# Second block's neighbourhood attention: TensorE's work on two tiles put together, VectorE's and GpSimd's finishing steps moved later

## The chip, the core and the metric

The kernel runs on one core of a Trainium2 chip. The core has five engines that run their own instruction streams in order and meet at semaphores: TensorE (PE, matrix products; PEld in the profile is its weight load), VectorE (DVE), ScalarE (ACT), GpSimd (POOL) and SyncE (SP, which only starts transfers here). The metric is the device time of one execution in microseconds (us), less is better.

## The reference, cut to what matters

Two blocks follow each other over 512 tokens of width 1024. The first (sparse attention beside a state-space mixer) isn't touched. The second has two layers; in each, 1024 columns of output are made by two attentions, a differential one (`out_b`) and a neighbourhood one (`out_a`), gated, and multiplied by `w_out`:

```python
def neighborhood_attention(q, k, v, rpb):   # 8 heads of 64, grid of 8 rows x 64 columns
    ...
        logits = jnp.einsum('bhcd,bhicjd->bhcij', qr, kr).astype(jnp.float32) * scale + bias[None]
        p = jax.nn.softmax(logits.reshape(b, h, GRID_W, wr * NA_WIN_C), axis=-1)
        ...
        return jnp.einsum('bhcij,bhicjd->bhcd', p, vr)
...
    y = jnp.concatenate([out_a * jax.nn.silu(g_a), out_b * jax.nn.silu(g_b)], axis=-1)
    x = x + y @ w_out[l]
```

Each query sees a window of 8 x 16 neighbours. The change concerns how `out_a` is worked through, and what stands around the start of `y @ w_out[l]`.

## The kernel before

**Tiles.** The neighbourhood attention of a layer is cut into 16 tiles (`PAIRS_NA`, `N_NA`): tile m is a block of 128 queries (i = m % 4) of a pair of heads (p = m // 4), each head with a window of 256 keys. One tile passes through six steps on four engines:

- scores (`na_score`, TensorE): per head three products, since q and k are kept as a high and a low part (`q_hi`, `q_lo`, `k_hi`, `k_lo`). The two heads lie on rows 0 to 63 and 64 to 127 of the array (64*128 in the trace). They go to two of four banks (`S_BANKS`), so that scores m wait until tile m-2 has been taken.
- take (`na_take`, VectorE): adds the bias and finds the maximum, into `prob2` (called `ring` in the trace). It waits for the bias of its pair of heads, which GpSimd's queue loads (`load_bias`).
- exponentials (`na_exp`, ScalarE), two per tile, then the reciprocal of the sums (`na_inverse`, VectorE) and the scaling (`na_scale`, GpSimd).
- turn (`na_turn`, TensorE, L1542 in the trace, 128*128): four transposes into bank 0 or 1; the move (`na_move`, ScalarE) takes them to `probT2` (`soft` in the trace).
- values (`na_weigh`, TensorE, 128*64): the products with v. The trace records eight for a tile, and names v `xn_t` or `v` according to the block. Two tiles, a *group* g, share a bank.
- products and low part: `na_out` (VectorE) multiplies a group by its gate twice, once rounded into `hT_hi` and once in full; `na_lo` (GpSimd) makes the rest, `hT_lo`. TensorE's products with `w_out` read both.

**Order.** Every engine's order is written out by hand. Tiles 0 to 2 (`N_EARLY`) are scored and taken while the last projections still run. From tile 3 on, TensorE does in step j: scores j, turn j-3 (`NA_LAG`), values j-4. VectorE does take j, reciprocal j-1, on odd j from 7 the products of group (j-7)//2, and on j = 6, 8, 10, 12 the low part of a quarter of the other attention's result (`mixT_lo`, L2161). ScalarE does move j-3, exponentials j, and on j = 4, 6, 8, 10 the high part of that quarter (`mixT_hi`). GpSimd scales tile m, and on even m from 6 makes the low part of group m//2 - 3; the last three low parts follow the last scale.

**End of the stage.** After step 16 TensorE does the first half of output tile 0 (`out_rows(0, 6, ...)`: twelve products that need the other attention only and the bank of tile 14's scores), then turn 14, values 13, turn 15, values 14 and 15, and the first half of output tile 1. Then it waits for `na_lo` of all groups (L1642) and does the second halves.

## Time and profile before

| | us |
|---|---|
| three runs | 935.77, 937.44, 937.67 |
| median | 937.44 |
| profiled execution | 937.15 |
| its span, first to last instruction | 935.3 |
| mean granted TensorE clock | 0.997 |

Busy in that span: PE 899.6 us (96%), PEld 707.5, DVE 578.1, ACT 449.5, POOL 116.9. The stage that the change touches runs twice, about 562 to 596 us and about 857 to 890 us into the span. How to read the rows: a time is the start, the number after it the duration in us; "x4" is the number of instructions merged in the row; a bracket at the end gives the idle time of the engine before the row and what ended it. A matmul's duration is longer than its pitch, since the engine overlaps them; the distance from one start to the next is what a step costs.

### The profile page before, as it was taken

To read this page: it belongs to the slowest core of one execution; us is meant where nothing else is said; L and a number is where in the kernel's file an instruction comes from. 1 tells how busy PE (TensorE), PEld (TensorE's weight loads), DVE (VectorE), ACT (ScalarE), POOL (GpSimd) and SP (SyncE) were. 2 spreads that over 40 slices of the span, in tenths; PEclk is the share of its full clock that TensorE was granted. 3 is DMA by queue.
4 is the path that set the end of the run, shared out by engine and by line. 5 is a ranking of instruction groups with operands and counts; after the bars stand their busy time and mean duration, and the time that the engine had idled before them with its cause. 6 is when DMAs were issued, how large, how long until landed. Compare 5 with 4: busy or idle time off the path is not lost.

```text
span 935.3 us, 14659 instructions
## 1 busy us (share of the span) xinstructions
PE 899.6 (96%) x5733; PEld 707.5 (76%) x5733; DVE 578.1 (62%) x1168; ACT 449.5 (48%) x962; POOL 116.9 (12%) x137
## 2 busy tenths in 40 slices
PE   3999999999999999999999999999999999999996
PEld 1679888774667788887788886788887778887785
DVE  5899798988886472438953447245255975335633
ACT  4634324566785243426925349234333863535731
POOL 1001120005300010000010017200000010002702
PEclk9999999999999999999999999999999999999998
DMA  9735636266000332322204334123242222323103
GB/s 381 314 99 131 187 137 181 102 187 242 22 2 1 113 128 92 113 90 88 90 22 138 105 94 133 43 90 91 90 138 95 78 91 90 90 90 120 62 23 90
DMA packets 34646, 104.69 MB, mean 112 GB/s; under 512 B 14929, under 2 KB 14929, under 8 KB 32146
## 3 DMA queue, kind: packets, MB, share of 16 engines
q1 hardware_dynamic: 28098, 85.77, 27.9%
q0 software_dynamic: 3824, 15.73, 5.3%
q10 hardware_dynamic: 2656, 2.26, 0.9%
q8 instruction: 46, 0.75, 0.3%
q14 instruction: 22, 0.18, 0.1%
HBM read 98.37 MB, written 4.19 MB: 110 GB/s over the span
## 4 chain that ended last, share of the span: by engine, by line
PE 88%; DVE 4%; ACT 3%; DMA 2%; issue 2%; POOL 0%; SPq 0%; POOLq 0%; DVEq 0%; ACTq 0%
PE bank L1043 81%; PE bank L1383 2%; PE bank L1403 2%; PE bank L1542 1%; DMA ring<-in_w_ada 1%; DMA bias_ring<-in_na_bias 1%; PE bank L1459 1%; DVE arena L1670 0%; PE bank L1449 0%; ACT ring L855 0%; ACT w_hi L903 0%; ACT arena L736 0%; DVE soft L2133 0%; DVE soft L2111 0%; DVE xn_t L2176 0%
## 5 line engine op out<-in xcount | busy, mean ns | idle before, releaser
L2156 DVE TENSOR_TENSOR w_lo<-ring,w_hi 128x1024 fp32r<-128x1024 f32 x80 | 97.8, 1225 | 114.6 <-ACT w_hi L903 111.6
L1043 PE MATMUL bank<-w_hi,hT_hi 128*128 128x512 f32 x320 | 125.6, 392 | 1.3 <-issue 1.0
L1043 PE MATMUL bank<-hT_hi,w_hi 128*128 128x512 f32 x320 | 126.2, 395 | 0.0
L1043 PE MATMUL bank<-w_lo,hT_hi 128*128 128x512 f32 x320 | 124.7, 390 | 0.0
L1043 PE MATMUL bank<-hT_hi,w_lo 128*128 128x512 f32 x320 | 124.6, 389 | 0.0
L1043 PE MATMUL bank<-hT_lo,w_hi 128*128 128x512 f32 x320 | 124.6, 389 | 0.0
L1043 PE MATMUL bank<-w_hi,hT_lo 128*128 128x512 f32 x320 | 124.5, 389 | 0.0
L903 ACT ACTIVATE w_hi<-ring 128x1024 fp32r<-128x1024 f32 x80 | 84.4, 1058 | 11.6 <-PE bank L1043 11.4
L1043 PEld LDWEIGHTS bank<-w_hi,hT_hi 128*128 128x128 f32 x320 | 60.1, 188 | 15.1 <-issue 2.9
L1043 PEld LDWEIGHTS bank<-hT_hi,w_hi 128*128 128x128 f32 x320 | 60.1, 188 | 14.0 <-issue 0.7
L1043 PEld LDWEIGHTS bank<-hT_lo,w_hi 128*128 128x128 f32 x320 | 60.1, 188 | 12.7
L1043 PEld LDWEIGHTS bank<-w_lo,hT_hi 128*128 128x128 f32 x320 | 60.1, 188 | 12.7
L1043 PEld LDWEIGHTS bank<-w_hi,hT_lo 128*128 128x128 f32 x320 | 60.1, 188 | 12.1
L1043 PEld LDWEIGHTS bank<-hT_hi,w_lo 128*128 128x128 f32 x320 | 60.1, 188 | 12.0
L908 ACT ACTIVATE bank<-x_t 128x512 f32<-128x512 f32 x24 | 14.5, 602 | 95.7 <-DVE x_t L2361 62.2
L566 POOL TENSOR_TENSOR ring<-ring,small 128x512 f32<-128x512 f32 x32 | 35.5, 1115 | 165.3 <-DVE small L2257 164.9
L855 ACT ACTIVATE ring<-ring,small 128x512 f32<-128x512 f32 x64 | 45.6, 714 | 13.9 <-DVE small L2101 11.4
L1043 PE MATMUL bank<-arena 128*64 128x64 f32 (+5 forms) x608 | 51.0, 293 | 0.3 <-PE bank L1043 0.2
L2101 DVE CUSTOM_DVE_ANT_0 ring<-bank,bias_ring 128x512 f32<-128x512 f32 x64 | 41.2, 685 | 0.0
L1043 PEld LDWEIGHTS bank<-arena 128*64 128x64 f32 (+1 forms) x608 | 31.3, 147 | 11.4 <-issue 10.2
L974 ACT ACTIVATE q_hi<-bank 128x512 fp32r<-128x512 f32 x16 | 9.6, 598 | 60.2 <-PE bank L1043 60.2
L2312 DVE SCALAR_TENSOR_TENSOR q_lo<-bank,q_hi 128x512 fp32r<-128x512 f32 x16 | 11.1, 692 | 43.2 <-ACT q_hi L974 43.2
(321 smaller groups left out, 1804.1 us busy)
## 6 DMA issues: line engine op xcount, KB each, us to landing
ring<-in_w_units SPq DMA_DIRECT2D x80, 512.0 KB, 3.7
ring<-in_w_ada SPq DMA_DIRECT2D x4, 2048.0 KB, 10.5
bias_ring<-in_na_bias POOLq DMA_DIRECT2D x8, 1024.0 KB, 5.4
ring<-in_w_out SPq DMA_DIRECT2D x2, 2048.0 KB, 8.6
bias_ring<-in_t_bias POOLq DMA_DIRECT2D x8, 448.0 KB, 3.7
x_t<-in_x SPq DMA_DIRECT2D x4, 512.0 KB, 5.7
arena<-in_w_ada SPq DMA_DIRECT2D x1, 2048.0 KB, 19.9
arena<-in_w_ada SPq DMA_DIRECT2D x2, 1024.0 KB, 22.8
```

The costliest lines, as they stand in the source:

```text
L566: pool.tensor_tensor(p, p, r, MUL).then_inc(S["na_scaled"], 1)
L855: act.activation(p, p, ACT.Exp, scale=-1.0, bias=negm[:, k % 8:k % 8 + 1], accum_out=ssum[:, k % 8:k % 8 + 1])\
L903: act.activation(w_hi[:, u % 4], raw_w[:, u % 4], ACT.Copy).then_inc(S["w_hi_ready"], 1)
L908: settle(act.activation(place[:, 0:n], x[:, i, c0:c0 + n], ACT.Square, scale=scale, accum_out=ssq[:, part * NT + i:part * NT + i + 1]))
L974: act.activation(q_hi[:, t, :], src[:, :], ACT.Copy, scale=SCALE).then_inc(S["qk_hi"], 1)
L1043: return pe.matmul(out, lhsT, rhs, start=first, stop=last)
L1383: ins = pe.transpose(bank[u % 2][:, b * P:(b + 1) * P], src[:, b * P:(b + 1) * P], ident)
L1403: ins = pe.transpose(bank[k % 2][:, b * P:(b + 1) * P], prob1_of(k)[:, b * P:(b + 1) * P], ident)
L1459: ins = pe.transpose(bank[ROW_BANKS[i][b]][:, k * P:(k + 1) * P], xn[:, i % 2, (4 * b + k) * P:(4 * b + k + 1) * P], ident)
L2101: dve.tensor_tensor_reduce(prob_of(k)[:, 0:width], bank[S_BANKS[k % 4]][:, 0:width], bias, -scale, 3.0e38, ADD, MIN, negm[:, k % 8:k % 8 + ...
L2156: dve.tensor_tensor(w_lo[:, u % 4], raw_w[:, u % 4], w_hi[:, u % 4].bitcast(fp32), SUB).then_inc(S["w_split"], 1)
L2312: dve.scalar_tensor_tensor(lo_[:, t, :], bank[(pt2(l, g) + t) % 4][:, :], SCALE if isq else 1.0, hi_[:, t, :].bitcast(fp32), MUL, SUB).the ...
```

## The change

Nothing is computed otherwise; four orders are altered, in both layers.

```diff
@@ GpSimd
                     na_scale(l, m)
-                    if m >= 6 and m % 2 == 0:
-                        na_lo(l, m // 2 - 3)
-                for g in range(N_NA // 2 - 3, N_NA // 2):
+                    if m >= 10 and m % 2 == 0:
+                        na_lo(l, m // 2 - 5)
+                for g in range(N_NA // 2 - 5, N_NA // 2):
                     na_lo(l, g)
@@ TensorE
-                        for j in range(N_EARLY, N_NA + NA_LAG + 1):
-                            if j < N_NA:
-                                na_score(l, j)
-                            if j <= N_EARLY + 1:
-                                pe.wait_ge(S["proj_evac"], pt2(l, 8) - 1 + j - N_EARLY)
-                            if j < N_NA + NA_LAG:
-                                na_turn(l, j - NA_LAG)
-                            if j > N_EARLY:
-                                na_weigh(l, j - NA_LAG - 1)
-                            if j == N_NA:
-                                out_rows(0, 6, range(0, 4))
+                        na_score(l, N_EARLY)
+                        pe.wait_ge(S["proj_evac"], pt2(l, 8) - 1)
+                        na_turn(l, 0)
+                        pe.wait_ge(S["proj_evac"], pt2(l, 8))
+                        for j in range(N_EARLY + 1, N_NA, 2):
+                            na_score(l, j)
+                            na_score(l, j + 1)
+                            for m in (j - NA_LAG, j + 1 - NA_LAG):
+                                na_turn(l, m)
+                            for m in (j - NA_LAG - 2, j - NA_LAG - 1):
+                                if m >= 0:
+                                    na_weigh(l, m)
+                        na_turn(l, N_NA - 3)
+                        na_turn(l, N_NA - 2)
+                        na_weigh(l, N_NA - 5)
+                        na_weigh(l, N_NA - 4)
+                        out_rows(0, 6, range(0, 4))
+                        na_turn(l, N_NA - 1)
+                        for m in (N_NA - 3, N_NA - 2, N_NA - 1):
+                            na_weigh(l, m)
                         out_rows(1, 7, range(0, 4))
@@ VectorE
-                            if j >= 7 and j % 2:
-                                na_out(l, (j - 7) // 2)
+                            if j >= 8 and j % 2 == 0:
+                                na_out(l, (j - 8) // 2)
                             ...
                         na_inverse(l, N_NA - 1)
-                        for g in range(N_NA // 2 - 3, N_NA // 2):
+                        for g in range(N_NA // 2 - 4, N_NA // 2):
                             na_out(l, g)
```

TensorE in the middle of the stage: before, one tile's scores, one turn, one tile's values, and the next scores.

```order
L1043 MATMUL bank<-k_hi,q_hi 128x256 x2
L1043 MATMUL bank<-k_hi,q_lo 128x256 x2
L1043 MATMUL bank<-k_lo,q_hi 128x256 x2
L1542 MATMUL bank<-cons,ring 128x128 x4
L1043 MATMUL bank<-soft,xn_t 64x128 x4
L1043 MATMUL bank<-k_hi,q_hi 128x256 x2
```

After, scores of two tiles, two turns, values of two tiles:

```order
L1043 MATMUL bank<-k_hi,q_hi 128x256 x2
L1043 MATMUL bank<-k_hi,q_lo 128x256 x2
L1043 MATMUL bank<-k_lo,q_hi 128x256 x2
L1043 MATMUL bank<-k_hi,q_hi 128x256 x2
L1043 MATMUL bank<-k_hi,q_lo 128x256 x2
L1043 MATMUL bank<-k_lo,q_hi 128x256 x2
L1542 MATMUL bank<-cons,ring 128x128 x8
L1043 MATMUL bank<-soft,v 64x128 x8
L1043 MATMUL bank<-k_hi,q_hi 128x256 x2
```

The scores of the second tile moved ahead of the turn, and the turns of two tiles stand together.

TensorE at the end of the stage, before: turn 13 and values 12, the first half of output tile 0 (`w_hi`, `w_lo`), then turn 14, values 13, turn 15, values 14, values 15, and output tile 1.

```order
L1542 MATMUL bank<-cons,ring 128x128 x4
L1043 MATMUL bank<-soft,v 64x128 x4
L1043 MATMUL bank<-w_hi,hT_hi 128x512
L1043 MATMUL bank<-w_hi,hT_lo 128x512
L1043 MATMUL bank<-w_lo,hT_hi 128x512
...
L1542 MATMUL bank<-cons,ring 128x128 x4
L1043 MATMUL bank<-soft,xn_t 64x128 x4
L1542 MATMUL bank<-cons,ring 128x128 x4
L1043 MATMUL bank<-soft,xn_t 64x128 x4
L1043 MATMUL bank<-soft,v 64x128 x4
L1043 MATMUL bank<-w_hi,hT_hi 128x512
```

After: turns 11 and 12, values 9 and 10, turns 13 and 14, values 11 and 12, then output tile 0, turn 15, values 13 and 14, values 15, and output tile 1.

```order
L1542 MATMUL bank<-cons,ring 128x128 x8
L1043 MATMUL bank<-soft,xn_t 64x128 x8
L1542 MATMUL bank<-cons,ring 128x128 x8
L1043 MATMUL bank<-soft,v 64x128 x8
L1043 MATMUL bank<-w_hi,hT_hi 128x512
L1043 MATMUL bank<-w_hi,hT_lo 128x512
L1043 MATMUL bank<-w_lo,hT_hi 128x512
...
L1542 MATMUL bank<-cons,ring 128x128 x4
L1043 MATMUL bank<-soft,xn_t 64x128 x8
L1043 MATMUL bank<-soft,v 64x128 x4
L1043 MATMUL bank<-w_hi,hT_hi 128x512
```

Turn 14 moved from behind the first half of output tile 0 to before it.

VectorE around tile 8, before: the reciprocal of tile 7, a low part of the other attention (L2161), the take of tile 9 (L2249, four rows), the reciprocal of tile 8 and the two products of a group (L2263, L2264).

```order
L2257 RECIPROCAL small<-small 128x2
L2161 TENSOR_TENSOR hT_lo<-y,hT_hi 128x512
L2249 ISA ring,small<-bank,bias_ring 128x256
L2249 ISA small 128x1
L2249 ISA ring,small<-bank,bias_ring 128x256
L2249 ISA small 128x1
L2257 RECIPROCAL small<-small 128x2
L2263 TENSOR_TENSOR hT_hi<-bank,y 128x256
L2264 TENSOR_TENSOR y<-bank,y 128x256
L2249 ISA ring,small<-bank,bias_ring 128x256
```

After, where the numbers of the lines are 9 higher: the reciprocal of tile 7, two products, the low part, the take of tile 9, the reciprocal of tile 8, the take of tile 10.

```order
L2266 RECIPROCAL small<-small 128x2
L2272 TENSOR_TENSOR hT_hi<-bank,y 128x256
L2273 TENSOR_TENSOR y<-bank,y 128x256
L2170 TENSOR_TENSOR hT_lo<-y,hT_hi 128x512
L2258 ISA ring,small<-bank,bias_ring 128x256
L2258 ISA small 128x1
L2258 ISA ring,small<-bank,bias_ring 128x256
L2258 ISA small 128x1
L2266 RECIPROCAL small<-small 128x2
L2258 ISA ring,small<-bank,bias_ring 128x256
```

The two products moved from behind an odd tile's take to behind the even one's, in front of the low part.

## Rows read from the trace of the kernel before

**Rows 1.** Page, part 4: shares of the chain that ended last, by engine.
```profile
PE 88%; DVE 4%; ACT 3%; DMA 2%; issue 2%; POOL 0%; SPq 0%; POOLq 0%; DVEq 0%; ACTq 0%
```

**Rows 2.** Timeline, TensorE, layer 2: start, length, engine, line, operation, operands, count.
```profile
869.43 0.38 PE L1043 MATMUL bank<-k_hi,q_hi 64*128 64x256 f32 x2
869.65 0.28 PE L1043 MATMUL bank<-k_hi,q_lo 64*128 64x256 f32 x2
869.77 0.28 PE L1043 MATMUL bank<-k_lo,q_hi 64*128 64x256 f32 x2
870.00 0.64 PE L1542 MATMUL bank<-cons,ring 128*128 128x128 f32 x4
870.57 0.66 PE L1043 MATMUL bank<-soft,xn_t 128*64 128x128 f32 x8
871.16 0.39 PE L1043 MATMUL bank<-k_hi,q_hi 64*128 64x256 f32 x2
```

**Rows 3.** Timeline, TensorE, three places elsewhere where one kind of work stands together.
```profile
555.14 0.38 PE L1043 MATMUL bank<-k_hi,q_hi 64*128 64x256 f32 x2
...
555.60 0.28 PE L1043 MATMUL bank<-k_hi,q_hi 64*128 64x256 f32 x2
...
556.04 0.50 PE L1043 MATMUL bank<-hT_hi,w_hi 128*128 128x512 f32 x1
...
643.56 1.91 PE L1459 MATMUL bank<-cons,xn_t 128*128 128x128 f32 x16
...
250.06 1.09 PE L1043 MATMUL bank<-arena,cols 128*64 128x128 f32 x16
```

**Rows 4.** Table by stretches: length, busy per engine (in order PE, PEld, DVE, ACT, POOL).
```profile
861.05:879.21 18.16, 17.93 (x185) 12.85 (x186) 14.08 (x67) 18.16 (x61) 16.17 (x17) 1.00 0.43 143
...
566.04:584.70 18.66, 17.77 (x184) 12.82 (x184) 14.24 (x64) 18.38 (x60) 16.89 (x18) 1.00 0.47 163
```

**Rows 5.** Timeline, TensorE, then ScalarE, start of the stage in layer 2.
```profile
860.42 0.39 PE L1043 MATMUL bank<-k_hi,q_hi 64*128 64x256 f32 x2 [0.72 <-DVE small L2249]
...
861.05 0.57 ACT L968 ACTIVATE soft<-bank 128x512 f32<-128x512 f32 x1
861.53 0.49 ACT L961 ACTIVATE ring<-ring,small 128x256 f32<-128x256 f32 x1
```

**Rows 6.** Timeline, TensorE, end of the stage in layer 2, then in layer 1.
```profile
881.10 0.50 PE L1043 MATMUL bank<-w_hi,hT_hi 128*128 128x512 f32 x1
...
883.96 0.60 PE L1542 MATMUL bank<-cons,ring 128*128 128x128 f32 x4
...
887.01 0.50 PE L1043 MATMUL bank<-w_hi,hT_hi 128*128 128x512 f32 x1
...
586.75 0.50 PE L1043 MATMUL bank<-w_hi,hT_hi 128*128 128x512 f32 x1
...
592.66 0.50 PE L1043 MATMUL bank<-w_hi,hT_hi 128*128 128x512 f32 x1
```

**Rows 7.** Timeline, GpSimd, layer 2: scale of tile 14, low part 4.
```profile
879.79 1.04 POOL L566 TENSOR_TENSOR ring<-ring,small 128x512 f32<-128x512 f32 x1 [0.34 <-DVE small L2257]
880.79 0.73 POOL L571 TENSOR_TENSOR hT_lo<-y,hT_hi 128x256 fp32r<-128x256 f32 x1
```

**Rows 8.** Timeline, VectorE: take 8 in layer 1; products and low part in layer 2.
```profile
573.19 0.42 DVE L2249 CUSTOM_DVE_ANT_0 ring<-bank,bias_ring 128x256 f32<-128x256 f32 x1 [1.29 <-DMA bias_ring<-in_na_bias]
...
869.64 0.40 DVE L2263 TENSOR_TENSOR hT_hi<-bank,y 128x256 fp32r<-128x256 f32 x1
...
870.29 0.41 DVE L2249 CUSTOM_DVE_ANT_0 ring<-bank,bias_ring 128x256 f32<-128x256 f32 x1
...
871.61 0.67 DVE L2161 TENSOR_TENSOR hT_lo<-y,hT_hi 128x512 fp32r<-128x512 f32 x1
872.20 0.42 DVE L2249 CUSTOM_DVE_ANT_0 ring<-bank,bias_ring 128x256 f32<-128x256 f32 x1
```

**Rows 9.** Waits of TensorE, 595 to 858 us: total, times, longest.
```profile
PE bank L1383 <- ACT soft L862: 1.4, 2, 0.9
```

## The prediction

> **What bounds the kernel now.** I read the chain of waits first: TensorE holds 88% of it [rows 1]. Then the timeline of TensorE through one attention stage, the table by stretches for ScalarE, and the rows where the two meet. The stage occurs twice (layer 1 at about 562 to 596 us, layer 2 at about 857 to 890), with 16 tiles each.
>
> In the middle of the stage one tile costs TensorE 1.73 us: scores 0.57 (869.43 to 870.00), a turn 0.57 (to 870.57), values 0.59 (to 871.16) [rows 2]. The scores are the place to look: three products of 256 columns start 0.22, 0.12 and 0.23 us apart. Where six of them stand in a row, the second three come 0.12 apart throughout: 0.46 for the first three, 0.44 to the next kind of work for the second three, 0.90 together against 2 x 0.57 [rows 3]. So a change of kind costs about 0.2 us. For turns: 16 transposes last 1.91 us [rows 3] and 4 last 0.64 [rows 2], so 12 more cost 1.27, 0.106 each, and four are 0.42 of a pitch of 0.57 to 0.59: the change costs about 0.16. For values, 16 products last 1.09 [rows 3] and 8 last 0.66 [rows 2]: 8 more are 0.43 of a pitch of 0.59, the change 0.16.
>
> But TensorE isn't alone. ScalarE is busy 18.16 us of the 18.16 between 861.05 and 879.21 in layer 2, and 18.38 of 18.66 in layer 1 [rows 4]. It does one move (0.48 from start to start) and two exponentials (0.49 each) per tile [rows 5], 1.46 us, and for four of the tiles a copy of a mixed part too. The chain runs through TensorE only because ScalarE, just as long, starts no later. This is the reading on which all else rests: **both have the same work in this stretch, and only TensorE's shrinks.**
>
> **The change, part by part, against the profiled execution** (937.15 us, 0.3 under the median of 937.44; shifts are added to the median).
>
> 1. *Kinds joined.* Per layer, 13 groups of scores become 7 (6 x 0.2 = 1.2 us), 16 of turns become 9 (7 x 0.16 = 1.1), 16 of values become 8 (8 x 0.16 = 1.3). TensorE's own work shrinks by 3.6 us a layer, a pair of tiles from 3.45 to 2.93. How much of it reaches the end is decided below.
>
> 2. *The start.* Before, turn 1 ran ahead of scores 5, which waited for VectorE until 860.42 [rows 5]; the move of turn 1 on ScalarE started at 861.05 [rows 5]. Now turn 1 stands behind scores 5: 860.42 + 0.55 + 0.59 = 861.56, and with about 0.1 of signalling the move starts at 861.65. ScalarE, full from there on, is 0.60 later. What is queued behind that move is every exponential from tile 4 on. In layer 1 the shift is the same, but 0.28 us of idle time in ScalarE's stretch [rows 4], where VectorE waited 1.29 for the bias transfer [rows 8], swallow it to 0.3.
>
> 3. *The end, where it decides.* Before, the first half of output tile 0 (2.86 us, 881.10 to 883.96 [rows 6]) needed only turns up to 13 ahead of it, and covered the scaling of tiles 14 and 15 on GpSimd. Now turn 14 stands ahead of it, then values 11 and 12. Turn 14 needs scale 14, which began at 879.79 and takes 1.04 [rows 7]. With 2. it begins at 880.39, ends 881.43; turn 14 from 881.5 to 882.1; two groups of values, 0.16 + 16 x 0.054 = 1.02, to 883.1. The output tile starts 2.0 us later than at 881.10.
>
> 4. *What comes back.* From the start of output tile 0 to that of output tile 1 it was 5.91 us (881.10 to 887.01, and 586.75 to 592.66 in layer 1) [rows 6]. Now it is 2.86 + one turn 0.58 + three groups of values 0.16 + 3 x 0.43 = 1.45, together 4.89: 1.0 back.
> So at least 2.0 - 1.0 = **+1.0** in layer 2, and 1.7 - 1.0 = **+0.7** in layer 1.
>
> 5. *VectorE's rows, the added wait.* Its two products of a finished group (0.40 and about the same) took 0.65 from start to the next row [rows 8], and the low part of a mixed tile 0.59 (871.61 to 872.20) [rows 8]. They stood after different tiles; now both stand after the same (even) tile, once the reciprocal of the odd tile before it has waited for its exponentials. Behind them are queued the next take (0.69) and, behind that, the even tile's reciprocal, which releases GpSimd. Counted from the end of exponentials 9, say, reciprocal 10 comes 0.1 + 0.65 + 0.59 + 0.69 = 2.0 later, though exponentials 10 were over after 1.5. TensorE waits for turn 10 behind that, and turn 9 and values 7 and 8 are around it. I went through the blocks of layer 2 with these durations: scores 10 at 870.3, 12 at 873.8, 14 at 877.2, so blocks of 3.4 to 3.6 us and not 2.93. Turn 11 ends at 879.1; ScalarE wanted it at 878.5, and idles 0.6. That goes straight on to scale 14: another **+0.6** in layer 2, and about +0.4 in layer 1. Bounds: 0, if the two works fit into the half microseconds in which VectorE waits for ScalarE anyway, and +1.2 a layer, which is both works in series (0.65 + 0.59) once, at the end.
>
> 6. *Low parts on GpSimd.* Two fewer stand among the scales (0.73 each [rows 7]), two more behind scale 15. GpSimd idled 0.34 ahead of scale 14 [rows 7], so this takes nothing off the path; at most it gives 5. some room. Behind scale 15, four of the five are done beside values 13 to 15 and the first half of output tile 1 (2.87 us); the last needs values 15, VectorE's 0.65, its own 0.73 and some 0.3 of signalling, which leaves 1.2 us of that cover. If that half weren't there, it would cost 1.6. Value: 0. The bias load is issued one low part earlier, 0.73 sooner; the take that waited was for the load before it, so 0.
>
> Behind the stage a delay stays: between 595 and 858 us TensorE's longest entry of waiting is 1.4 us, for ScalarE [rows 9], so no transfer there absorbs it.
>
> **Sum.** Layer 2: +2.0 - 1.0 + 0.6 = +1.6. Layer 1: +1.7 - 1.0 + 0.4 = +1.1. Together +2.7: 937.44 + 2.7 = **940.1 us**. Of this case alone the bounds are +1.7 (5. at zero) and, with 5. at 1.2 a layer, 1.7 + 2.4 = +4.1: 939.1 to 941.5.
>
> A rule to weigh here: the Trainium skill, "TensorEngine Tiling (Array Packing)", Key Properties, says that changing the tiling mode drains the engine, while changing the tile within a mode doesn't. The three kinds have three modes in the rows (64x128, 128x128, 128x64), and the 0.16 to 0.2 us at each change agree with it. Taken alone it says that the change gains 3.6 us a layer; that is the first rival.
>
> **Rivals.**
> *A. TensorE alone sets the end: faster.* For it: the chain names TensorE nearly throughout. Its price is 3.6 us less a layer, of which at most 0.6 goes at the start: 2 x 3.0 less, 931.4 us. Against it: ScalarE's 18.16 of 18.16 [rows 4], and that scale 14 can't run before exponentials 14. The point from which it decides: output tile 1 started at 887.01, its new stretch is 4.89, so output tile 0 must start before 882.12, turn 14 by 880.5, scale 14 end 0.4 earlier than before. That takes a ScalarE faster than in the trace. A part of it, -2 to -4 us, is likelier than the whole. Together 12%.
> *B. The start's delay is swallowed and the stalls of 5. don't come: no measurable difference.* Then a layer is +1.35 (turn 14 and two values behind scale 14: 880.83 to 882.5 instead of 881.10) less 1.0 = +0.3 to +0.8: 938.0 to 939.1. For it: the waits of VectorE for ScalarE before each reciprocal are slack. Against it: nothing lies between turn 1 and ScalarE's full stretch. 27%.
> *C. The new order of VectorE serialises.* Values 4 and 8 wait for the products of the group two before, which now come one tile later; if both works end up in series in more than one block, a layer costs +2.5: 942.4. For it: in layer 1 VectorE is already late by the bias transfer just there [rows 8]. Against it: after the mixed copies end ScalarE needs only 1.46 us a tile. 11%.
> *D. The joining saves nothing where it is done* (the second scores wait for the take of the tile before, the second turn for its scale, and the engine has emptied by then). Then the end pays 0.16 four times more a layer (turn 14, values 12, 14 and 15), 2 x 0.64: 941.4. It lies within the forecast's own bounds and is counted with it.
>
> **Chances.** Forecast, with D: 50%; A 12%; B 27%; C 11%. A measurement of this kernel can tell about 0.2%, 1.9 us, from no change. Faster by more: 12%. Within: 27% of B, and nearly none of the forecast's, whose lower end is +1.7: 28%. Slower by more: 60%. The range runs from 935.8, which cuts off most of A, to 942.0, which takes in D and the bounds of 5. and leaves out the most of C's upper half.
>
> **What would show it.** Right: TensorE's joined scores at a pitch of 0.90 for six; ScalarE's first move after exponentials 3 starts 0.5 to 0.6 later; a wait of TensorE for GpSimd ahead of turn 14, and output tile 0 starting 2 to 3 us later than at 881.10; 4.9 us from there to output tile 1. Wrong: ScalarE showing its exponentials of tile 15 over before 880.8, or output tile 0 starting before 882.1 (then A), or VectorE's products of even tiles preceding their waits (then 5. is 0).

## The result, and the profile after

The changed kernel is slower. Five runs of each on one chip: before 937.44 us (935.77 to 939.22), after 943.63 us (942.39 to 944.77); ratio 1.006, 95% interval 1.0049 to 1.007. The forecast was 940.1, and its range ended at 942.0. The profiled execution of after took 943.27 us with a span of 941.5, against 937.15 and 935.3, so the two profiles hold the whole difference.

Timeline of TensorE, layer 2, the end of the stage after; it answers to [rows 6]:

```profile
886.67 0.63 PE L1542 MATMUL bank<-cons,ring 128*128 128x128 f32 x4 [0.68 <-POOL ring L566]
887.23 1.10 PE L1043 MATMUL bank<-soft,v 128*64 128x128 f32 x16
888.26 0.50 PE L1043 MATMUL bank<-w_hi,hT_hi 128*128 128x512 f32 x1
...
891.12 0.60 PE L1542 MATMUL bank<-cons,ring 128*128 128x128 f32 x4
...
893.11 0.50 PE L1043 MATMUL bank<-w_hi,hT_hi 128*128 128x512 f32 x1
```

Turn 14 (886.67) waits for its scale, two groups of values follow, output tile 0 starts at 888.26 and output tile 1 at 893.11. I measure everything from scores 5 (863.38 after, 860.42 before), because what came earlier in the span, layer 1 above all, shifts layer 2 only as a whole:

| layer 2, us after scores 5 | before | after | shift | forecast |
|---|---|---|---|---|
| ScalarE's move of turn 1 | 0.63 | 1.73 | +1.10 | +0.6 |
| scale 14 (GpSimd) | 19.37 | 22.11 | +2.74 | +1.2 |
| output tile 0 | 20.68 | 24.88 | +4.20 | +2.6 |
| output tile 1 | 26.59 | 29.73 | +3.14 | +1.6 |

In layer 1 the last row reads 27.26, 30.39, +3.13 against +1.1, and the first row +0.61. The two layers make 6.27 us, about the difference of the spans (6.2). The excess over the forecast is there at scale 14 already; behind scale 14 all went as worked out. So the search is for what delays scale 14. Timeline of ScalarE, the same stretch of after:

```profile
865.11 0.60 ACT L968 ACTIVATE soft<-bank 128x512 f32<-128x512 f32 x1 [1.01 <-PE bank L1542]
...
876.07 0.60 ACT L968 ACTIVATE soft<-bank 128x512 f32<-128x512 f32 x1 [0.41 <-PE bank L1542]
...
882.03 0.51 ACT L961 ACTIVATE ring<-ring,small 128x256 f32<-128x256 f32 x1 [0.45 <-DVE small L2258]
...
883.63 0.60 ACT L968 ACTIVATE soft<-bank 128x512 f32<-128x512 f32 x1 [0.51 <-PE bank L1542]
```

ScalarE, which idled nowhere in [rows 4], now waits 1.01 us for turn 1 and then three times, 1.37 in all. What it waits for goes back to VectorE. Timeline of VectorE, layer 1 (answers to [rows 8]), and under it GpSimd beside it, then GpSimd in layer 2:

```profile
574.13 0.40 DVE L2272 TENSOR_TENSOR hT_hi<-bank,y 128x256 fp32r<-128x256 f32 x1
574.45 0.41 DVE L2273 TENSOR_TENSOR y<-bank,y 128x256 f32<-128x256 f32 x1
574.78 1.11 DVE L2170 TENSOR_TENSOR hT_lo<-y,hT_hi 128x512 fp32r<-128x512 f32 x1
575.82 0.41 DVE L2258 CUSTOM_DVE_ANT_0 ring<-bank,bias_ring 128x256 f32<-128x256 f32 x1
```

```profile
574.31 1.03 POOL L566 TENSOR_TENSOR ring<-ring,small 128x512 f32<-128x512 f32 x1 [0.24 <-DVE small L2266]
576.74 1.04 POOL L566 TENSOR_TENSOR ring<-ring,small 128x512 f32<-128x512 f32 x1 [1.40 <-DVE small L2266]
...
878.37 1.04 POOL L566 TENSOR_TENSOR ring<-ring,small 128x512 f32<-128x512 f32 x1 [1.40 <-DVE small L2266]
...
882.50 1.04 POOL L566 TENSOR_TENSOR ring<-ring,small 128x512 f32<-128x512 f32 x1 [1.40 <-DVE small L2266]
```

Two things stand here. Products, low part and the next take come in one piece, and the reciprocal behind them (576.50) is what the scale waits 1.40 us for. And the low part, 0.67 us before, takes 1.11: it starts after the scale, whose end is at 575.34, and ends 0.55 later. So it goes with the three low parts of a layer that stand behind products (takes 8, 10 and 12): they take 1.11, 1.10 and 1.89 us in layer 1 and 1.10, 1.10 and 1.26 in layer 2. The first of each layer, at take 6, has no products ahead of it and stays at 0.67.

One more thing was not in the forecast. Table by stretches, after (columns as in [rows 4]; the last three are granted clock, DMA share and GB/s):

```profile
862.00:864.00 2.00, 0.62 (x7) 0.46 (x7) 2.00 (x9) 0.99 (x4) 0.38 (x1) 0.96 0.25 47
864.00:866.00 2.00, 2.00 (x12) 1.67 (x12) 0.94 (x7) 0.99 (x4) 1.47 (x2) 0.50 0.82 248
866.00:868.00 2.00, 2.00 (x21) 1.53 (x21) 0.33 (x2) 2.00 (x8) 1.04 (x1) 0.69 0.81 307
```

Since turn 1 no longer stands ahead of scores 5, TensorE idles 1.55 us there instead of 0.72 [rows 5], and then the granted clock is 0.50 (the level of 1.2 GHz) for about 3 us: turns 1 and 2 take 1.97 us. In layer 1, after 1.54 us of idling, the clock falls too, but over a microsecond later, when turns 1 and 2 are done: they take 1.09 us there, and the move of turn 1 comes 0.61 us late and not 1.10.

### The profile page after: what moved, and what is told of

Its sections match the earlier page's. It is cut to its first block, busy times and chain, and to the rows that moved or that the text cites. A ratio compares the mean times of both kernels' runs of the same rounds, so it can differ in the third digit from the quotient of the medians.

```text
span 941.5 us, 14660 instructions
## 1 busy us (share of the span) xinstructions
PE 898.9 (95%) x5733; PEld 709.6 (75%) x5733; DVE 581.6 (62%) x1168; ACT 450.2 (48%) x962; POOL 115.3 (12%) x137
## 4 chain that ended last, share of the span: by engine, by line
PE 87%; DVE 5%; ACT 3%; issue 2%; DMA 1%; POOL 0%; SPq 0%; POOLq 0%; DVEq 0%; ACTq 0%
PE bank L1043 81%; PE bank L1383 2%; PE bank L1403 2%; PE bank L1542 1%; DMA ring<-in_w_ada 1%; ACT ring L961 1%; PE bank L1459 1%; DVE hT_lo L2170 0%; DVE arena L1679 0%; DVE ring L2258 0%; PE bank L1449 0%; ACT ring L855 0%; ACT arena L736 0%; DVE soft L2142 0%; DVE soft L2120 0%
## 5 line engine op out<-in xcount | busy, mean ns | idle before, releaser
L1043 PEld LDWEIGHTS bank<-arena 128*64 128x64 f32 (+1 forms) x608 | 31.3, 147 | 11.4 <-issue 10.4
```

Source lines behind the costliest of these rows:

```text
L1043: return pe.matmul(out, lhsT, rhs, start=first, stop=last)
```

## The experiments

Each kernel has one profile and was timed against the kernel before on the same chip (938.3 to 938.6 us there). Differences in us are the ratio less 1, times 938.4; the 95% interval of the ratio stands behind it, and is 0.8 to 1.3 us to either side in most runs. The changed kernel itself was timed on another chip, against five runs of before with the median 937.44; against the 938.4 of the others its 943.63 us would be +5.2, and not the +5.6 of its ratio.

### Which engine's edit costs the time

**pe**: TensorE's part of the diff alone, the other engines as before.

> TensorE's edit alone, VectorE's and GpSimd's orders as before. Theory E (the terms of the end and the start are right, about +1.0 and +0.7 us a layer, and GpSimd's edit is worth nothing): +1.2 to +2.0 us against the kernel before, that is as much as TensorE's and GpSimd's edits together (+1.2). Rival G (GpSimd's edit gives TensorE's edit its room: with the low parts among the scales the scales come 0.7 later where TensorE waits for them): +2.5 us or more, with TensorE's longest waits for GpSimd's scale over 0.6 us.

Measured: 940.19 us, ratio 1.0022 (1.0014 to 1.003), +2.1. That lies between the two expectations; the trace decides for theory E. From scores 5 to output tile 1 it takes 28.05 and 27.45 us, +0.79 and +0.86, together +1.65 for the forecast's +1.7 of steps 2 to 4, and TensorE waits for GpSimd 0.6 us at the longest.

**pool**: GpSimd's part alone.

> GpSimd's edit alone. My term for it was 0, and so within 0.5 us of the kernel before. Rival: fewer low parts among the scales let the scales start earlier where TensorE waits for them (0.64 us once in layer 1): -0.5 to -1 us; or the three last low parts keep TensorE waiting ahead of the second half of the output tiles: +1 us or more.

Measured: 938.01 us, 0.9997 (0.9988 to 1.0006). Nothing, as forecast.

**dve0**: the changed kernel with VectorE's order of before.

```diff
-                            if j >= 8 and j % 2 == 0:
-                                na_out(l, (j - 8) // 2)
+                            if j >= 7 and j % 2:
+                                na_out(l, (j - 7) // 2)
```

> The changed kernel with VectorE's order of before (products on odd steps, three groups at the end); TensorE's and GpSimd's orders stay changed. Theory S: every low part 0.67 (one up to 0.9), no wait of TensorE for VectorE's take 13, and 939.5 us (938.5 to 941.0), still slower than before because turn 14 stands ahead of output tile 0 and turn 1 behind scores 5. Rival O expects about the same, since its work in series is gone too; a rival T (TensorE's order alone is the loss) expects 943 or more.

Measured: 939.88 us, 1.0013 (1.0005 to 1.0022), +1.2. So of the loss of 5.6 VectorE's edit makes 4.4 by the ratios, 3.8 by the medians and by the profiles (from scores 5 to output tile 1, both layers: 60.12 against 56.30 us). The low part is back at 0.67, and the same step of VectorE reads:

```profile
873.75 0.17 DVE L2266 RECIPROCAL small<-small 128x2 f32<-128x2 f32 x1 [0.48 <-ACT ring L961]
873.83 0.67 DVE L2170 TENSOR_TENSOR hT_lo<-y,hT_hi 128x512 fp32r<-128x512 f32 x1
874.42 0.42 DVE L2258 CUSTOM_DVE_ANT_0 ring<-bank,bias_ring 128x256 f32<-128x256 f32 x1
```

**vec**: VectorE's part alone, on the kernel before.

> VectorE's edit alone: the products of a group move from the odd take to the even one, in front of the low part; TensorE and GpSimd as before. Theory O (the two works on one tile serialise whatever TensorE's order): at least +3 us against the kernel before, and VectorE's low part of 1.1 us and more where GpSimd scales beside it. Rival P (it needs TensorE's pairs: only because values come in pairs does VectorE fall behind): within +1 us.

Measured: 956.87 us, 1.0206 (1.0182 to 1.023), +19. Theory O so far as it says that VectorE's edit is bad by itself, and P is out; but the low parts that are seen last 0.67 to 0.68, so it is not their length. Waits of TensorE in layer 1 and the table by stretches:

```profile
PE bank L1043 <- DVE y L2264: 4.7, 5, 1.9
```

```profile
572.00:576.00 4.00, 2.15 (x18) 1.49 (x16) 2.19 (x8) 3.62 (x12) 2.41 (x3) 0.80 0.00 1
...
584.00:588.00 4.00, 3.69 (x22) 2.40 (x20) 1.82 (x12) 1.85 (x6) 1.04 (x1) 0.50 0.01 2
...
600.00:604.00 4.00, 3.49 (x15) 2.43 (x14) 1.48 (x5) 0.70 (x3) 2.95 (x4) 0.50 0.24 66
```

Values 4 wait 1.85 us for the products of group 0, which share their bank. From then on the granted clock is 0.50 for some 30 us (574.5 to 605), into the first half of output tile 0. In layer 2 the wait is 1.86 us, the five waits for y make 7.1 us, and the clock stays at 1.00 all the same. This separates the two, for this one execution (961.41 us, 4.5 above the median): from scores 5 to output tile 1 layer 2 takes 33.99 us, 7.4 more than before, and layer 1 43.44, 16.2 more. The waits are worth about 7 us a layer, and 9 us more came where the clock was down. That the joined order of TensorE softens VectorE's edit (+4.4 instead of +19) I had not thought of: values 4 stand behind the scores of two more tiles there.

### What it is in VectorE's edit

**swap**: the changed kernel, on even takes the low part first and then the products.

```diff
-                            if j >= 8 and j % 2 == 0:
-                                na_out(l, (j - 8) // 2)
                             if j - MIX_LAG in MIX_AT:
                                 m = MIX_AT.index(j - MIX_LAG)
                                 mixT_lo(l, m, 4 + m, mixT[m])
+                            if j >= 8 and j % 2 == 0:
+                                na_out(l, (j - 8) // 2)
```

> The changed kernel, with one swap on VectorE: on even steps the low part of the other attention's quarter stands before the two products of a group again (the order is then reciprocal, low part, products). Theory S (shared access): in the changed kernel the low part lasts 1.10 to 1.89 us in six of eight places because it comes while GpSimd's scale runs; put first, it begins before the scale and lasts 0.67 again in at least six of eight, GpSimd's scale beside it grows to 1.4, and the kernel falls from 943.6 to 941.0 (940.2 to 942.0). Rival O (only the sum of work between two reciprocals counts, the order within it doesn't): low part still over 1 us, or 0.67 with the time unchanged, 943.0 to 944.2.

Measured: 943.29 us, 1.0045 (1.0031 to 1.0059), +4.2. Rival O's side: the low part is back at 0.67 in six of eight places (0.75 in two), and the time isn't. TensorE's waits in layer 2 show what came instead:

```profile
PE bank L1043 <- DVE y L2273: 2.0, 3, 0.9
```

Then it is either that both works meet behind one take, or that the products come a take later. Three runs for that:

**late**: the changed kernel, products at j = 9, 11, 13, 15.

```diff
-                            if j >= 8 and j % 2 == 0:
-                                na_out(l, (j - 8) // 2)
+                            if j >= 9 and j % 2:
+                                na_out(l, (j - 9) // 2)
```

> The changed kernel with the products of a group one take later still, behind the odd take (j = 9, 11, ...), so that products and low part stand on different tiles again, as before, while values meet the products even later. Theory O (it is the meeting of both works on one tile): +0.5 to +2 us against the kernel before, low parts at 0.67 us. Rival L (it is the lateness of the products, which the values of the group two on wait for): +6 us or more, with TensorE waiting for VectorE's product (y) over 1 us in several places of a layer.

Measured: 950.94 us, 1.0128 (1.0113 to 1.0144), +12. Rival L so far as lateness by itself can cost: all low parts are at 0.67, and TensorE waits for y 5.4 us in layer 1, 2.2 at the longest.

**odd**: the products as changed (even takes), the low parts at j = 7, 9, 11, 13.

```diff
-                            if j - MIX_LAG in MIX_AT:
-                                m = MIX_AT.index(j - MIX_LAG)
+                            if j - MIX_LAG - 1 in MIX_AT:
+                                m = MIX_AT.index(j - MIX_LAG - 1)
```

> The changed kernel with the low parts of the mixed tiles one take later (j = 7, 9, 11, 13), so that they stand on the odd tiles and the products, unmoved, on the even ones. Theory O (the loss is the meeting of products and low part behind one take): what is left are TensorE's own terms, +1.0 to +2.0 us against the kernel before, low parts at 0.67 us. Rival L (the loss is that the products come a take later, and the values of the group two on wait for them): +4 us or more, as the changed kernel.

Measured: 942.05 us, 1.0045 (1.0032 to 1.0058), +4.2. Rival L's time. Seven of the eight low parts are at 0.67 as expected; the last of layer 1 lasts 2.68, so this run isn't lateness alone.

**same**: dve0 with that same edit, so that products and low part are together, on the odd takes, and the products not late.

> Products back behind the odd take, as before, and the low parts moved to the odd takes as well, right behind the products: together, but not late. TensorE's and GpSimd's edits kept. Theory O (meeting is the loss): +4 us or more against the kernel before. Rival L (lateness is the loss): +1 to +2 us, as with VectorE's order of before (+1.2).

Measured: 941.55 us, 1.0036 (1.0024 to 1.0049), +3.4. Neither expectation: between them. All four corners, TensorE and GpSimd as changed; the first number is by the ratio, the second how much longer scores 5 to output tile 1 is than before in the two layers' profiles together:

| us against before | products not late | products a take later |
|---|---|---|
| low part on other tiles | +1.2, +2.5 (dve0) | +4.2, +3.9 (odd) |
| low part behind them | +3.4, +3.6 (same) | +5.6, +6.3 (changed) |

(The profile shown of before is a quick one, 1.2 us under the medians of the other chips, so the second numbers stand higher.) Against dve0, `odd` costs 3.0 by the times and 1.4 by the profiles, `same` 2.2 and 1.1, the changed kernel 4.4 and 3.8. That `odd` and `same` are each slower than dve0 is clear of the noise; neither of my two theories was the whole. But the corners aren't the prices of lateness and of meeting alone, for three reasons. In `odd` and `same` the low part, too, comes a take later than before. The long low part of `odd` belongs to holding, not to lateness. And TensorE's granted clock fell behind scores 5 in both layers in the profiles of dve0 and the changed kernel, in one layer in that of `same` and in none in that of `odd`. If the three moves simply add up, which no run shows, the late products are worth 2.6 us by the times (2.1 by the profiles), the meeting 1.8 (1.8), and the late low part 0.4 (-0.6); these are estimates from the four corners.

In `same` the low part reads 1.10 to 1.11 us seven times and 2.11 once, so it is held there as in the changed kernel; in `odd` TensorE waits for y 1.4 us in layer 1 and 0.7 in layer 2.

**nolow**: the changed kernel, with the low parts of the mixed tiles cut to 16 of 512 columns.

```diff
-                dve.tensor_tensor(cut(hT_lo[:, f, :], i=NT, t=P), src, ...
+                dve.tensor_tensor(cut(hT_lo[:, f, :], i=NT, t=P)[:, :, 0:4], src[:, :, 0:4], ...
```

> The changed kernel, with the low parts of the mixed tiles cut to four columns of each 128 (the rest is left out), so that they cost VectorE about 0.1 us and not 0.67 to 1.9. Theory O: +1 to +2 us against the kernel before. Rival L: +3.5 us or more, with TensorE waiting for VectorE's product y.

Measured: 942.07 us, 1.004 (1.0027 to 1.0054), +3.8. That is rival L's side, but the run did not take away what it was to take away, and this is its finding. VectorE, and the scale beside it:

```profile
873.48 0.59 DVE L2170 TENSOR_TENSOR hT_lo<-y,hT_hi 128x16 fp32r<-128x16 f32 x1
873.99 0.41 DVE L2258 CUSTOM_DVE_ANT_0 ring<-bank,bias_ring 128x256 f32<-128x256 f32 x1
```

```profile
873.00 1.03 POOL L566 TENSOR_TENSOR ring<-ring,small 128x512 f32<-128x512 f32 x1 [0.84 <-DVE small L2266]
```

A subtraction of 16 columns lasts 0.59 us beside a scale, and 0.15 (at 868.25) ahead of one. It ends at 874.07, 0.04 after the scale. So it isn't slowed, it is held until GpSimd's instruction is over. Cut to a thirty-second, the subtraction still costs 0.58 or 0.59 us in five of eight places, and 1.12 in one.

### The start, the end and the clock

**start**: the changed kernel with turn 1 ahead of scores 5.

```diff
                             na_score(l, j)
+                            if j == N_EARLY + 1:
+                                na_turn(l, 1)
                             na_score(l, j + 1)
```

> The changed kernel with turn 1 before scores 5 again in step 4 (scores 4, turn 1, scores 5, turn 2, values 0). Theory C (start and clock): TensorE's granted clock stays at 1.00 in the 5 us behind scores 5 in both layers (0.50 for about 3 us in the changed kernel), the move of turn 1 follows exponentials 3 without a gap, and the kernel falls by 1 us a layer to 941.6 (941.0 to 942.4). Rival (the first delay is swallowed by later waits for VectorE): 943.0 to 944.2 with the clock at 1.00.

Measured: 943.95 us, 1.0046 (1.0033 to 1.0058), +4.3. The time is the rival's; from the changed kernel it can't be told apart with certainty (0.3 us more by the medians, 1.3 less by the ratios, 1.1 less from scores 5 to output tile 1 in the profiles), so whether VectorE's stalls swallow the delay stays open. The move of turn 1 is back at 0.64 us behind the start of scores 5 in both layers. One sign of the expectation failed: in layer 2 the clock fell to 0.50 for about 3 us all the same, after 0.97 us of idling. **dve0s** is the same edit where VectorE's stalls are gone:

> VectorE's order as before, TensorE's and GpSimd's edits kept, and turn 1 back in front of scores 5. If my term for the start is right (0.60 us in layer 2, 0.3 in layer 1, carried by ScalarE to the end), -0.9 us against the kernel without this step: +0.3 us against the kernel before, from scores 5 to output tile 1 27.9 and 27.4 us. Rival (it is swallowed there too): +1.2, 28.2 and 28.0 us.

Measured: 937.79 us, 0.9997 (0.9987 to 1.0007), -0.3, so 1.5 less than dve0 (with an interval of about 1.2 us); from scores 5 to output tile 1 it takes 26.84 and 27.09 us for 28.25 and 28.05. There the term is real. Whether it is larger than my 0.9 can't be said: in dve0's profile the clock fell in both layers and the move of turn 1 came 2.03 and 1.30 us behind the start of scores 5, here the clock stays at 1.00 and the move comes at 0.63, so the gain holds the clock as well.

**keep**: the changed kernel with scores 4 done three times more, without a signal, to fill the idle time of TensorE.

```diff
+                            for _ in range(3 if j == N_EARLY + 1 else 0):
+                                na_score(l, j, False)
                             na_score(l, j)
```

> The changed kernel, with the products of scores 4 made four times in place of once (the first three not counted by the semaphore and written over), so that TensorE works through 1.1 of the 1.5 us in which it waits for take 3. It separates the clock from turn 1's place. Theory C: clock 1.00 behind scores 5, turns 1 and 2 in 1.03 us and not 1.5 to 1.9; the move of turn 1 still 0.5 to 0.6 late. If the clock costs much of the loss: 941.5 to 942.5. If it lies mostly under other waits: 943.0 to 943.8. I take 942.9.

Measured: 943.49 us, 1.0044 (1.0031 to 1.0057). The stretch where the clock had been 0.50 reads now:

```profile
864.00:866.00 2.00, 1.53 (x16) 1.27 (x14) 1.87 (x12) 1.35 (x5) 1.24 (x2) 1.00 0.60 137
```

The clock is at its upper level there in both layers, the move of turn 1 comes 1.25 us behind the start of scores 5 in both (0.61 later than before, my term for the start), and the time is hardly less: in this place the 3 us at 1.2 GHz cost nothing that can be told.

**t14**: dve0 with turn 14 behind the first half of output tile 0, next to turn 15.

```diff
                         na_turn(l, N_NA - 3)
-                        na_turn(l, N_NA - 2)
                         na_weigh(l, N_NA - 5)
                         na_weigh(l, N_NA - 4)
                         out_rows(0, 6, range(0, 4))
+                        na_turn(l, N_NA - 2)
                         na_turn(l, N_NA - 1)
```

> VectorE's order as before, TensorE's and GpSimd's edits kept, but turn 14 back behind the first half of output tile 0, in front of turn 15. If my term for the end is right (turn 14 ahead of the output tile waits for scale 14: 0.6 us of waiting and 0.45 of work ahead of it), the output tile starts 1.0 us earlier in each layer and the stretch behind it is 0.42 to 0.48 longer: -0.5 to -0.6 us a layer, so 0.0 to +0.5 us against the kernel before, where the kernel with turn 14 ahead had +1.2. Rival W (values 13 wait there for the move of turn 14 and 15 instead): no gain over it, +1.2.

Measured: 938.34 us, 1.0003 (0.9994 to 1.0012), +0.3, 0.9 less than dve0. By the times that isn't clear of the noise (about 1.2 us); the profile shows the term: output tile 0 starts 1.5 and 1.0 us earlier behind scores 5 than in dve0, and the stretch to output tile 1 is 0.43 and 0.44 longer (5.29 for 4.86 and 4.85), as expected.

### A version that beats both

**tail**: the kernel before, and the end alone rewritten.

```diff
-                        for j in range(N_EARLY, N_NA + NA_LAG + 1):
+                        for j in range(N_EARLY, N_NA + 1):
...
+                        na_turn(l, N_NA - 2)
+                        na_turn(l, N_NA - 1)
+                        for m in (N_NA - 3, N_NA - 2, N_NA - 1):
+                            na_weigh(l, m)
```

> The kernel before, with one thing of the change alone: behind the first half of output tile 0 turns 14 and 15 stand together, then values 13, 14 and 15; turn 14 stays behind it. Theory K (joined kinds pay where ScalarE no longer sets the pace): three changes of kind less, 0.16 to 0.2 us each, and values 13 out of the way: -0.5 to -0.6 us a layer, -1.0 to -1.2 in all. Rival W (TensorE waits there for scale 15 or the move of turn 15 anyway): 0 to -0.3 in all.

Measured: 936.77 us, 0.9984 (0.9976 to 0.9993), -1.5. Output tile 0 to 1 takes 5.33 us in both layers (587.58 to 592.91, 882.31 to 887.64), for 5.91 [rows 6]. **t14s** is TensorE's joined order with both ends put right (turn 1 and turn 14), VectorE as before:

> TensorE's joined order with VectorE's order as before, turn 1 back in front of scores 5 and turn 14 back behind the first half of output tile 0. If the two terms add up (-1.5 us for the start and -1.2 for the end, from +1.2): -1.5 us against the kernel before. If ScalarE's work caps them (ScalarE was full in the stretch before): -0.5 us or less.

Measured: 936.2 us, 0.9976 (0.9966 to 0.9987), -2.3.

In these profiles VectorE's wait for the bias ahead of take 8 ([rows 8]: 1.29) is anything from 0 to 1.7 us. **bias** loads the bias of that pair of heads in two halves, columns 0 to 511 of each head (tiles 8 and 9) before scale 2, the rest before scale 3, and takes 8 and 9 wait for the first alone:

```diff
+                    if m == 2:
+                        load_half(l)
```

> The kernel before with the bias of heads 4 and 5 loaded in two halves, the first issued before scale 2. Tail with this was -2.9 us and tail alone -1.6, so by the difference -1.3 us (-0.5 to -2) against the kernel before, and no wait for the transfer ahead of take 8. If tail and bias only work together (because the end was hidden by the transfer's delay): within 0.5 us.

Measured: 937.49 us, 0.9986 (0.9978 to 0.9995), -1.3, no such wait. With tail, **tailbias**:

> The kernel before with turns 14 and 15 and values 13 to 15 together behind the first half of output tile 0 (as run tail, -1.6 us), and the bias of heads 4 and 5 loaded in two halves, the first issued before scale 2 instead of all before scale 3. If VectorE's wait for that transfer (0.6 to 1.5 us ahead of take 8) is on the path by what ScalarE then lacks, 0.3 to 0.9 us a layer: -2.2 to -3.2 us against the kernel before. If ScalarE absorbs it: -1.6 us.

Measured: 935.57 us, 0.9969 (0.9958 to 0.998), -2.9. And with t14s, **joinbias**:

> TensorE's joined order with turn 1 ahead of scores 5 and turn 14 behind output tile 0 (as t14s, -2.1 to -2.3 us), VectorE's order as before, GpSimd's low parts as changed, and the bias in two halves. If both gains add up: -3.3 to -3.6 us against the kernel before, 26.0 us or less from scores 5 to output tile 1 in both layers. If ScalarE's work is the floor (13 tiles of 1.46 us and four copies of 0.57 between its first move and the last exponentials): no better than tail with bias, -2.9 us.

Measured: 935.81 us, 0.9968 (0.9956 to 0.998), -3.0: no better than tailbias. Table by stretches, tailbias and then joinbias:

```profile
862.00:880.00 18.00, 17.79 (x184) 12.71 (x182) 14.38 (x65) 18.00 (x60) 15.61 (x17) 1.00 0.28 93
```

```profile
862.00:880.00 18.00, 16.76 (x190) 12.97 (x188) 14.42 (x65) 18.00 (x59) 14.88 (x14) 1.00 0.28 90
```

TensorE has 1.03 us less to do in the second, ScalarE is busy 18.00 of 18.00 in both, and output tile 0 starts at 880.63 and 880.55, 20.69 and 20.75 us behind scores 5. That is the sentence "only TensorE's work shrinks" in two rows. The times alone don't exclude that the gains add up to -3.3. And in layer 1 of joinbias the clock fell behind scores 5, after 0.97 us of idling, and output tile 0 comes at 21.45 us, for 20.67 in tailbias: here, where little waiting for VectorE lies behind it, a fall of the clock may well have cost the 0.8 us that in keep it didn't.

## Why the prediction was wrong

- *What bounds the kernel.* Right, and shown by the two rows above: ScalarE is as long as TensorE in the stage, and joining frees only TensorE.
- *1, kinds joined.* The sizes were right (one count was off by one: before, values stood in 15 groups, since 14 and 15 were together already): six products of the joined scores take 0.91 us (870.00 to 870.91), 16 values 1.02 (868.98 to 870.00), for 0.90 and 1.02. Its worth in the middle of the stage is nothing that can be told (joinbias against tailbias), as said; at the end it is 0.58 a layer (tail).
- *2, the start.* Right in mechanism and size: the move came 0.61 us late in layer 1, and in both layers of keep. The +1.10 of layer 2 has the fallen clock in it, which I did not see coming. What it costs in the changed kernel can't be told (start); without VectorE's edit it is 1.5 us with the clock's share (dve0s against dve0).
- *3 and 4, the end.* Right: output tile 0 starts 2.77 us after scale 14 (2.7 by my times), and from there to output tile 1 it is 4.85 (4.89). TensorE's edit alone measures +1.65 in the profile and +2.1 by the ratio, for +1.7. The 4.85 also rules out D.
- *5, VectorE's rows.* **The step that failed.** +0.6 and +0.4 us were forecast, +1.0 in all, with a bound of 1.2 a layer, 2.4 in all; 4.4 were measured by the ratios and 3.8 by the profiles (2.1 and 1.7 in the layers). I priced the two works once, in series (0.65 + 0.59). But the pile recurs at the takes of tiles 8, 10 and 12, the scale behind it waits 1.40 us each time, and the low part takes 1.02 to 1.82 us from its start to the next row and not 0.59, since it now comes while GpSimd works. By my times scores 10, 12 and 14 should begin 9.9, 13.4 and 16.8 us behind scores 5 in layer 2; they begin at 10.4, 14.3 and 17.8. And I counted a lateness of the products only in rival C, at two places of a layer; swap, odd and late show TensorE waiting for y where no low part is held (2.0 us in layer 2 of swap). How the 4.4 divide between meeting, holding and lateness is an estimate only (the corners above).
- *6, GpSimd.* Right, zero.
- *Rivals.* C named the mechanism nearest to what happened, and at 942.4 it was still 1.2 too low. A and B needed slack in ScalarE or in VectorE: ScalarE had none, and the half microseconds of VectorE ahead of its reciprocals weren't enough.

On the held low part the Trainium skill, "SBUF — State Buffer", section "SBUF: two separate sides", has the rule that I should have weighed: an operation of VectorE with two inputs in SBUF and one of GpSimd that reads SBUF take a shared pair of ports as an exclusive lock, and the one that starts later is blocked for the whole of the other. The trace agrees in both directions: the low part is held when the scale is first (0.59 us for 16 columns), and in the kernel before, where the low part was first, it was the scale that grew (below). How long VectorE can be held where GpSimd's instructions follow without a gap is shown below, too.

## What to carry to other kernels

Before making one engine's work cheaper, look for a second engine that is busy without a gap in the same stretch. Here there was one, and only the ends of the stretch gained: a five-line edit there gained 1.5 us where the rewrite of the whole lost 5.6. An instruction that is moved "one place later, since it isn't urgent" has to be priced at each place where it recurs, by who waits for the instruction behind it and by what runs beside it on the engine that shares its ports. Where two causes are suspected, run all four corners, and look in each trace whether the run moved anything else: here two corners also moved the low part, and one of them had it held for 2 us, so that the division stayed an estimate.

## What the runs showed of the hardware that I had not expected

Where VectorE's subtraction and GpSimd's scale overlap, the one that starts first runs at full speed. In the kernel before, where the low part starts at 871.61 and lasts 0.67 [rows 8], GpSimd reads:

```profile
871.77 2.51 POOL L566 TENSOR_TENSOR ring<-ring,small 128x512 f32<-128x512 f32 x2 [0.23 <-DVE small L2257]
```

Two scales in 2.51 us where two undisturbed ones take 2.05: 0.46 more, about what was left of the low part at 871.77 (0.51). After the change the same pair costs VectorE 0.44 instead (1.11 less 0.67), at a place where the other engines wait for VectorE.

The longest low part of the changed kernel, in layer 1, doesn't fit into that sentence. VectorE, and GpSimd beside it:

```profile
582.20 1.89 DVE L2170 TENSOR_TENSOR hT_lo<-y,hT_hi 128x512 fp32r<-128x512 f32 x1
```

```profile
581.85 0.61 POOL L555 DMA_DIRECT2D bias_ring<-in_t_bias  x1
582.49 1.05 POOL L566 TENSOR_TENSOR ring<-ring,small 128x512 f32<-128x512 f32 x1
```

It starts 0.29 us ahead of the scale, while GpSimd still issues a load, and yet it ends at 584.09, 0.55 after the scale, as if it had started behind it. In `odd` the same low part starts at 582.09 during two scales; GpSimd's low part follows them without a gap and ends at 584.22, and VectorE's ends at 584.77, again 0.55 later: 2.68 us. In `same` it lasts 2.11 us and ends 0.56 after GpSimd's low part. So one subtraction can be held over more than one instruction of GpSimd. It isn't always: at 578.19 in `same` it takes 1.10 us behind a scale, and GpSimd's low part, queued behind that scale, takes 1.18 instead of 0.73. Which of the two goes next these runs don't settle.

The granted clock can't be told from the idle time alone. Ahead of scores 5 TensorE's idle time depends on the kernel's order and is the same in both layers, so the 20 profiles can be compared there. After 0.72 us (before, pool, tail, bias, tailbias, vec) the clock stayed at 1.00 for the next 7 us and more in all 12 cases. After 0.96 or 0.97 us (start, dve0s, t14s, joinbias) it fell to 0.50 in 2 of 8. After 1.54 or 1.55 us it fell in 12 of 18: in both layers of the changed kernel, dve0, swap and t14, in one layer each of pe, same, nolow and late, and in none of odd. In keep, with 0.47 us, it stayed up. In the changed kernel it was back after about 3 us, and hidden. In vec it fell in layer 1, after 1.85 us of waiting for y, and stayed down for 30 us with further waits of 0.5 to 0.8 us about every 7 us; in layer 2, with waits of 1.15 to 1.86 us about every 5 us, it didn't fall at all. What decides it, these runs don't show.

The same holds elsewhere: around 720 to 740 us, where TensorE idles 1.07 us in the profiles of before, after, pool, keep, same and nolow, the granted clock of that stretch is 1.00 in the first two and 0.91 in the other four, and there the stretch between the two attention stages is 1.0 us longer. This is a reason why single profiles of this kernel differ by 1 us.
